# Two layers of a hybrid decoder trunk on one core: another order of the setup, an output tail by row blocks, and a later place for one small sum

## The reference, cut to what matters

```python
for l in range(2):                                   # 512 tokens, 1024 channels
    mod = silu(c) @ ada_w[l] + ada_b[l]              # 9 rows of 1024: shift, scale, gate, three times
    h = rms_norm(x, ffn1_norm[l]) * (1 + sc1) + sh1
    x = x + 0.5 * g1 * ((silu(h @ Wg) * (h @ Wu)) @ ffn1_w_out[l])
    h = rms_norm(x, mix_norm[l]) * (1 + sc2) + sh2   # 8 heads, two softmax maps each, with a
    ...                                              # relative bias; conv of 31 taps; two gates
    x = x + g2 * (merged @ w_mix_out[l])
    h = rms_norm(x, ffn2_norm[l]) * (1 + sc3) + sh3
    x = x + 0.5 * g3 * ((silu(h @ Wg) * (h @ Wu)) @ ffn2_w_out[l])
return rms_norm(x, final_norm)
```

## Time and profile before

| | |
|---|---|
| runs | 2573.01, 2574.42, 2575.19 us (median 2574.42) |
| profiled execution | 2577.65 us, its span 2576.0 us |
| PE busy in the span | 2514.0 us |
| DVE, ACT, POOL busy | 1675.6, 966.4, 115.8 us |
| chain that ended last, PE's share | 84% |

### The profile page before, as it was taken

One profiled execution on the slowest core, in us unless ns is written; L12 is line 12 of the kernel. 1 busy time (PEld: TensorE's weight loads), 2 busy tenths in 40 slices (PEclk: granted clock), 3 DMA queues, 4 the chain that ended last, 5 costly groups with the idle time before them and its releaser, 6 DMA issues.

```text
span 2576.0 us, 34560 instructions
## 1 busy us (share of the span) xinstructions
PE 2514.0 (98%) x11378; PEld 2033.8 (79%) x11378; DVE 1675.6 (65%) x2493; ACT 966.4 (38%) x1625; POOL 115.8 (4%) x186
## 2 busy tenths in 40 slices
PE   5899999999999999999999999999999999999997
PEld 4788887777778888888878888877777888788886
DVE  6555578798988675543365557778989865643333
ACT  3222323545444343232243232255455443423222
POOL 2100010000000000000000001100000000000000
PEclk7899999999999999999999999999999999999998
DMA  6655475232232334543335555722232233333332
GB/s 215 182 161 157 148 237 160 81 87 82 84 89 83 101 120 131 161 125 93 103 89 158 161 163 188 228 78 84 83 87 80 86 98 98 90 94 95 96 96 94
DMA packets 470157, 311.97 MB, mean 121 GB/s; under 512 B 10723, under 2 KB 447205, under 8 KB 470084
## 3 DMA queue, kind: packets, MB, share of 16 engines
q1 hardware_dynamic: 445078, 227.63, 30.4%
q0 software_dynamic: 22144, 78.40, 9.4%
q10 hardware_dynamic: 2878, 5.20, 0.7%
HBM read 306.46 MB, written 5.05 MB: 121 GB/s over the span
## 4 chain that ended last, share of the span: by engine, by line
PE 84%; DVE 8%; issue 3%; ACT 3%; DMA 1%; ACTq 0%; POOL 0%; DVEq 0%; POOLq 0%; SPq 0%
PE bank L1307 26%; PE bank L1309 25%; PE bank L1308 25%; PE bank L1498 2%; DVE ada_acc L853 1%; PE bank L1477 1%; ACT w_hi L418 1%; DVE rstd L732 1%; DVE w_lo L715 1%; PE bank L1469 1%; DVE scaled L743 1%; DVE h_lo L752 1%; PE bank L1329 1%; DMA bias_rows<-bias_row 1%; PE bank L1334 0%
## 5 line engine op out<-in xcount | busy, mean ns | idle before, releaser
L715 DVE TENSOR_TENSOR w_lo<-w_raw,w_hi 128x1024 fp32r<-128x1024 f32 (+1 forms) x432 | 520.0, 1204 | 562.9 <-ACT w_hi L418 562.4
L1307 PE MATMUL bank<-h_hi,w_hi 128*128 128x512 f32 x2112 | 840.0, 398 | 9.1 <-DVE scaled L993 9.0
L1309 PE MATMUL bank<-h_hi,w_lo 128*128 128x512 f32 x2112 | 824.1, 390 | 0.0
L1308 PE MATMUL bank<-h_lo,w_hi 128*128 128x512 f32 x2112 | 823.8, 390 | 0.0
L418 ACT ACTIVATE w_hi<-w_raw 128x1024 fp32r<-128x1024 f32 (+1 forms) x432 | 449.5, 1041 | 864.1 <-PE bank L1309 807.0
L1307 PEld LDWEIGHTS bank<-h_hi,w_hi 128*128 128x128 f32 x2112 | 397.3, 188 | 100.2 <-issue 18.8
L1309 PEld LDWEIGHTS bank<-h_hi,w_lo 128*128 128x128 f32 x2112 | 397.0, 188 | 84.3
L1308 PEld LDWEIGHTS bank<-h_lo,w_hi 128*128 128x128 f32 x2112 | 397.7, 188 | 77.9 <-issue 0.5
L1097 DVE SCALAR_TENSOR_TENSOR conv_part<-glu,conv_taps,conv_part 128x512 f32<-128x512 f32 x464 | 318.9, 746 | 0.0
L1307 PE MATMUL bank<-s_hi,w_hi 128*128 128x512 f32 x704 | 274.6, 390 | 0.0
L1309 PE MATMUL bank<-s_hi,w_lo 128*128 128x512 f32 x704 | 274.0, 389 | 0.0
(11 more groups left out here) (199 smaller groups left out, 2535.1 us busy)
## 6 DMA issues: line engine op xcount, KB each, us to landing
w_raw<-in_ffn_w_in SPq DMA_DIRECT2D x176, 512.0 KB, 3.8
ada_raw<-in_ada_w POOLq DMA_DIRECT2D x128, 512.0 KB, 4.9
w_raw<-in_w_mix_in SPq DMA_DIRECT2D x112, 512.0 KB, 3.7
w_raw<-in_ffn_w_out SPq DMA_DIRECT2D x64, 512.0 KB, 3.8
w_raw<-in_ffn_w_out SPq DMA_DIRECT2D x32, 384.0 KB, 3.4
w_raw<-in_w_mix_out SPq DMA_DIRECT2D x18, 512.0 KB, 3.7
ada_first<-in_ada_w POOLq DMA_DIRECT2D x16, 512.0 KB, 10.8
w_raw<-in_w_attn_branch SPq DMA_DIRECT2D x16, 512.0 KB, 3.8
```

Source lines behind the costliest of these rows:

```text
L715: dve.tensor_tensor(wlo[slot][:, 0:n, :], raw[slot][:, 0:n, :], whi[slot][:, 0:n, :].bitcast(F32), ALU.subtract).then_inc(w_lo[slot], 1)
L1307: pe.matmul(acc, wh, hi[:, k0 + k, :], start=first and k == 0, stop=False)
L1308: pe.matmul(acc, wh, lo[:, k0 + k, :], start=False, stop=False)
L1309: mm = pe.matmul(acc, wl, hi[:, k0 + k, :], start=False, stop=last and k == n - 1)
```

## The change

Five things move:

- **POOL** issues all 16 pieces of `ada_first` and the lambda rows in one run, with no wait for `w_raw` between them; `row_rstd` comes behind them. The bias rows no longer wait for `lam_dots`.
- **Setup order.** PE turns the rows of x first, and makes the bias rows behind them; DVE does its two steps for that table (`bias_table`) after its fourth `first_step`. ACT splits the first two slabs ahead of `running_sum`. PE does `first_sum(0)` ahead of `norm_mean`. DVE splits slab 0 behind `scale_columns`.
- **ACT** waits for the bias rows and issues its two DMAs behind the whole tile loop of the first FFN; the copy itself is awaited only behind the norm of the mixing stage.
- **Group sums** in `ffn1_out` stand before block 5 of slab 5.
- **Tail.** The last `ffn2_out` is written out four times instead of a loop. In it ACT multiplies each finished tile of x by the gain (`out_gain`), PE turns it (`turn_rows`, 7 tiles within the slabs), ACT copies it (`out_copy`), all without the norm. The mean squares come as one column per 128 tokens: PE multiplies blocks of `running_sum` by a column of 1/1024 (`token_sums`), and behind the last slab those of the last square. ACT takes the root of 128x4, DVE the reciprocal, DVE and ACT scale the rows by it, and SP writes four DMAs of 512 KB. The unused last pair is gone.

```diff
 @@ gpsimd
             pool.dma_start(ADA0[:, k, D:2 * D], w_ada[:, k, D:2 * D]).then_inc(sem(f"ada0_scale{k}"), 16)
-        pool.wait_ge(sem("minus_half"), 1)
-        pool.wait_ge(sem("row_var"), 1)
-        pool.tensor_tensor(row_rstd[:, :], row_var[:, :], minus_half[:, :].to_broadcast([P, QB]), ALU.pow)\
-            .then_inc(sem("row_rstd"), 1)
-        for s in range(2):
-            pool.wait_ge(w_raw[s], 16)
         for k in range(KT):
             pool.dma_start(ADA0[:, k, 0:D], w_ada[:, k, 0:D]).then_inc(sem(f"ada0_shift{k}"), 16)
...
+        pool.wait_ge(sem("minus_half"), 1)
+        pool.wait_ge(sem("row_var"), 1)
+        pool.tensor_tensor(row_rstd[:, :], row_var[:, :], minus_half[:, :].to_broadcast([P, QB]), ALU.pow)\
+            .then_inc(sem("row_rstd"), 1)
...
         pool.wait_ge(sem("ada0_step"), 2 * KT)
-        pool.wait_ge(sem("lam_dots"), 2 * DEPTH)
         pool.wait_ge(sem("br_copied"), 2)
 @@ scalar
+        for s in range(2):
+            w_hi_part(0, s)
         act.wait_ge(sem("ssum_clear"), 1)
         act.wait_ge(sem("row_rstd"), 1)
         for t in range(QB):
             act.activation(SSUM[:, t * P:(t + 1) * P], ident[:, :], ACT.Copy, scale=row_rstd[:, t:t + 1]).then_inc(sem("row_sums"), 1)
-        for s in range(2):
-            w_hi_part(0, s)
...
                 ffn_tile(1, False, TP[0])
+                with act.Fori(2, FT) as i:
+                    ffn_tile(i)
                 if l == 0 and w == 0:
                     act.wait_ge(sem("br_out"), 16 * HEADS)
...
-                with act.Fori(2, FT) as i:
-                    ffn_tile(i)
...
+                            if last:
+                                out_gain(i * 2 + m // 3)
...
+                        if last and m == 5:
+                            out_copy(i * 2)
+                        if last and m == 2 and i:
+                            out_copy(i * 2 - 1)
 @@ tensor
+        def turn_rows(j):
+            pe.wait_ge(sem("y_gained"), j + 1)
+            if j >= 2:
+                pe.wait_ge(sem("y_copied"), j - 1)
+            for t in range(QB):
+                mm = pe.transpose(TP[j % 2][:, t * P:(t + 1) * P], T[j % 2][:, t * P:(t + 1) * P], ident[:, :])
+            mm.then_inc(sem("yt_ready"), 1)
+        def token_sums():
+            pe.wait_ge(sem("ssum_add"), DEPTH * 3 * KT - 1)
+            for t in range(QB):
+                pe.matmul(AUX[:, t:t + 1], SSUM[:, t * P:(t + 1) * P], invd[:, 0:1], start=t == 0, stop=False)
...
+                    if w == 0:
+                        extra[5] = {5: lambda: mod_sum_parts(seq + 1)}
+                    if last:
+                        extra[4] = {2: lambda: turn_rows(i * 2)}
+                        if i:
+                            extra[1] = {2: lambda: turn_rows(i * 2 - 1)}
+                        if i == KT // 2 - 1:
+                            extra[5] = {4: token_sums}
...
-                             at={2: lambda: mod_sum_parts(seq + 1)} if w == 0 and m == 5 else {})
+                             at=extra.get(m, {}))
```

More of the change, by code:

```diff
@@ L328, in _ @@
                             slab(pair + PAIR0[name] + i, t, cols(wt, l * KT, 8, i * (2 * P) + t * P + c0))
-        for s in range(2):
[L331 to L339, removed]
-        for s in range(2):
-            sp.wait_ge(w_raw[s], 16 * (DEPTH * PAIRS + 1))
+        for n in range(QB):
+            t = n // 2 + 2 * (n % 2)
+            sp.wait_ge(sem("y_last"), QB)
+            sp.wait_ge(sem(("y_scaled_dve", "y_scaled_act")[n % 2]), n // 2 + 1)
+            sp.dma_start(out[0, t * P:(t + 1) * P, :], YO[:, t, :]).then_inc(sem("y_out"), 16)
+        sp.wait_ge(sem("y_out"), 16 * QB)
     @block.gpsimd
@@ L507, in _ @@
             plain_hi(0, j)
+        act.wait_ge(sem("aux_ready"), 1)
+        act.activation(RSTD[:, :], AUX[:, :], ACT.Copy, scale=float(D)).then_inc(sem("aux_read"), 1)
         for s in range(2):
@@ L543, in _, with out_pair @@
                     load_bias_tile(0)
-                with act.Fori(2, FT) as i:
-                    ffn_tile(i)
-                if l == 0 and w == 0:
                     act.wait_ge(sem("lam_dots"), 2 * DEPTH)
-                    act.wait_ge(sem("br_again"), 16)
                     act.activation(lam_exp[:, :], lam_dot[:, :], ACT.Exp).then_inc(sem("lam_exps"), 1)
-                with act.Fori(0, KT // 2) as i:
+                last = l * 3 + 1 + 2 * w == DEPTH * 3
+                def out_pair(i):
                     for m in range(6):
@@ L699, in _ @@
                         plain_hi(l * 3 + 2, i * 2 + t)
[L702 to L706, removed]
+        act.wait_ge(sem("y_means"), 1)
+        act.activation(yroot[:, :], AUX[:, 0:QB], ACT.Sqrt, bias=eps[:, 0:1]).then_inc(sem("y_root"), 1)
+        act.wait_ge(sem("y_rstd"), 1)
+        for t in (2, 3):
+            act.activation(YO[:, t, 0:D - P], YO[:, t, 0:D - P], ACT.Copy, scale=yrstd[:, t:t + 1]).then_inc(sem("y_scaled_act"), 1)
         act.wait_ge(sem("bt_in"), 16 * (DEPTH * HEADS + 1))
@@ L1046, in _, with out_pair @@
                 clear_sum()
-                with dve.Fori(0, KT // 2) as i:
+                last = l * 3 + 1 + 2 * w == DEPTH * 3
+                def out_pair(i):
                     for m in range(6):
@@ L1068, in _ @@
                         chunk_columns(l, i * 2 + (4 + 2 * CHUNKS_IN[0]), seq + 1)
+                if last:
+                    for i in range(KT // 2):
+                        out_pair(i)
+                else:
+                    with dve.Fori(0, KT // 2) as i:
+                        out_pair(i)
                 if w == 1:
@@ L1415, in _ @@
         first_sum(0).then_inc(sem("scale0_summed"), 1)
+        norm_mean(0, 0)
         pe.wait_ge(sem("pt_ready"), 1 + DEPTH)
@@ L1455, in _ @@
                              k0, OUTG[g], g == 0, g == 2,
-                             at={2: lambda: mod_sum_parts(seq + 1)} if w == 0 and m == 5 else {})
+                             at=extra.get(m, {}))
+                if last:
+                    for i in range(KT // 2):
+                        out_pair(i)
+                else:
+                    with pe.Fori(0, KT // 2) as i:
+                        out_pair(i)
                 if w == 1:
@@ L1579, in _ @@
                              ready=lambda k: pe.wait_ge(sem("m_lo"), l * KT + k + 1))
-        norm_mean(DEPTH * AUXN, DEPTH * 3 * KT)
-        for j in range(KT):
-            pe.wait_ge(sem("unit_t"), DEPTH * UNITS + j + 1)
-            if j >= 2:
-                pe.wait_ge(sem("y_ready"), j - 1)
-            for t in range(QB):
-                mm = pe.transpose(TP[j % 2][:, t * P:(t + 1) * P], T[j % 2][:, t * P:(t + 1) * P], ident[:, :])
-            mm.then_inc(sem("yt_ready"), 1)
+        pe.wait_ge(sem("sq_ready"), DEPTH * 3 * KT)
+        for t in range(QB):
+            mm = pe.matmul(AUX[:, t:t + 1], SQ[:, t * P:(t + 1) * P], invd[:, 0:1], start=False, stop=t == QB - 1)
+        mm.then_inc(sem("y_means"), 1)
+        turn_rows(KT - 1)
     ctx.close()
```

101 lines of the change are left out of this document (65 added, 36 removed).

## The result

The changed kernel takes **2561.7 us** (median of 5 runs, 2560.63 to 2562.82) against 2574.47 of the kernel before; the ratio is 0.9949, with a 95% interval of 0.9936 to 0.9963. In time that is 13.1 us less (9.5 to 16.5), where 17.2 were forecast: the forecast time, 2557.2, missed by 4.5 us, and the range of 2552 to 2563 holds the measured one. The profiled execution took 2561.09 us, its span 2559.4.

What follows compares the result with a forecast made beforehand. PE, with 84% of the chain, was taken as the bound. Setup plus 4.1, stall minus 10.7, group sums minus 4.2 and tail minus 6.4 gave minus 17.2: 2574.4 to 2557.2 us, range 2552 to 2563 (8 in 10: 2549 to 2567).

Steps and rivals of the forecast that it cites:

- The stall: First FFN: PE's 8.1 us wait goes, and the low clock behind it (2.6 us): minus 10.7 us.
- The setup: Setup: the shift's 4096-byte packets starve the first slabs' 512-byte ones, `h_hi` starts at 38.9, not 34.80: plus 4.1 us.
- the last 0.08 MB take 0.3 us: Setup: after the shift's end at 35.1 us, SP's queue finishes slot 1's data by 35.4; semaphore at 36.6.
- The rule named in the prediction: Skill's DMA page: each DMA engine takes queues in turn by packet, not bytes; by it the sum is minus 17.2 us.
- The group sums: `ffn1_out`: sums three blocks later no longer wait, 8 times 0.53 us: minus 4.2 us.
- The tail: Last `ffn2_out` and end: PE gets 4.05 us more, the end comes 10.5 us sooner: minus 6.4 us.
- The 17.2: Whole kernel: the us saved by the sum of setup, stall, group sums and tail, from 2574.4 to 2557.2 us.
- The two signs of the setup: Setup: ACT's second `w_hi` starts at 36 to 37 us with a wait for `w_raw`; `h_hi` at about 39.
- no wait of over 1 us: Sign of being right: PE has no wait over 1 us between the shift's sums and the tail.
- B: Rival, setup: first slabs not starved, `h_hi` at some 31.8 us, setup minus 3.0, sum minus 24.3, 2550 us; chance 0.13.
- C: Rival, first FFN: the stall moves, as a slab beside the bias rows lands late; 2562 to 2568 us; chance 0.17.
- D: Rival: PE's clock stays low behind the shift's sums; decides from 86 matmuls, at 150 plus 13, 2587 us; chance 0.02.

Runs made afterwards that it cites:

- the second execution: The kernel before, unchanged, profiled a second time: ratio 0.9999 (0.9989 to 1.0008), span 2574.9 us.

## Why the prediction was right, and where it was off

**The stall, forecast minus 10.7.** Right in sum. The table has minus 10.94 against the profiled execution, of which 8.1 are the wait and the rest the low clock behind it. But that execution had a longer stall than the other four that have one (14.79 against 12.77 to 13.27 us), so the usual gain there is 8.9 to 9.4, and the part alone measured minus 10.0 (6.4 to 13.6). What the prediction had not told apart is which edit does it. It is POOL's `lam_dots` wait: moved alone, it removes the stall (minus 9.0), and putting ACT's wait back costs nothing once POOL issues early. The third edit, ACT's wait for `br_again` behind the stage, guards against a new wait: without it 2.3 us are lost in `ffn1_out`.

**The setup, forecast plus 4.1.** The mechanism was right, equal packets and unequal bytes, and it was the only part that costs time; the term was undersized, at plus 5.8 in the traces and plus 5.7 (3.3 to 8.0) alone. The step that was off is "the last 0.08 MB take 0.3 us", with the 1.2 us behind it (their row gives 1.1): it let SP's queue run free once the shift was through, at 35.1, and took the 16 DMA engines as one. The queues from 35 to 36 us:

```profile
DMA packets 338, 0.26 MB, mean 259 GB/s; under 512 B 80, under 2 KB 261, under 8 KB 338
q0 software_dynamic: 153, 0.17, 79.8%
q1 hardware_dynamic: 185, 0.09, 41.2%
```

POOL's queue still held packets: the lambda rows stand in its list behind the shift, 0.26 MB in all that the trace has as 128 packets of 2048 bytes, and the sum had left them out. At the 385 GB/s of this stage they are some 0.7 us, an estimate. But slot 1 was there only at 38.59, its split came at 38.61 and not at 36.6, and the trace shows more. The slab's semaphore is raised 16 times, once for each part, in the changed kernel first at 35.01, four times by 35.3, and for the last eight parts from 37.8 to 38.59. On the average the sum was good: before 36 us SP's queue had started as many packets as both slabs have. But the parts ended 3.6 us apart (3.9 with the setup part alone), and packets of the next slab, issued at 31.05, already went out before slot 1 was there. With the shift kept back they ended 1.2 us apart. So beside the shift the queue moves on unevenly, and a slab counts when its last part is there. Why it is uneven, and how the 2 us divide between this and the lambda rows, no run shows. From the split to `h_hi` it took 2.13 us, 2.3 forecast.

The true size may be larger still. Against the five runs in which the old setup has its first slab at 35.13 to 35.79, the setup part's 42.45 is 6.7 to 7.3 us later, within the interval of its run alone.

The rule named in the prediction, from the Trainium skill's page DMA: Bandwidth & Descriptors, section Queues, rings and completion order (queues take turns by packet), agrees with the counts wherever all queues have work: 566 and 564 with two queues, 484, 479 and 481 with three. The page's packet is a group of descriptors; whether the profile counts the same thing is not shown.

**The group sums, forecast minus 4.2.** Minus 4.2 in the table (2.0 and 2.2), minus 4.1 (1.8 to 6.4) alone. The time from start to start was the right measure; the table of waits had shown 1.8.

**The tail, forecast minus 6.4.** PE got 4.4 us more in the last `ffn2_out` (4.05 forecast), and the end came 11.05 us sooner (10.5 forecast): minus 6.65, or minus 6.4 against the second execution. The part alone measured minus 5.9 (3.3 to 8.2). The first output DMA came 5.4 us behind the start of the last matmul, 5.5 by the prediction's sum.

**The sum.** Trace against trace it came out at minus 16.6, and at minus 15.5 against the second execution. The four parts alone add up to 5.7 - 10.0 - 4.1 - 5.9 = -14.3. The medians of the whole differ by 12.8, its ratio gives 13.1 (9.5 to 16.5), and the run with ACT's wait in its old place, which is the same in time, gave 13.9. So of the 4.5 us by which 2557.2 missed, 1.7 are the undersized setup and up to 1.8 a stall read from one execution in which it was longer than usual; the rest is within what the measurement can tell. The 17.2 itself lies just outside the measured 9.5 to 16.5. The prediction's range is also not quite what its bounds give: with plus 2 to plus 6, 1.8 to 4.2 and minus 4 to minus 8 it is 2553.5 to 2563.9, which holds the result as well.

**The signs.** The group sums, the end and the missing stall came as said. The two signs of the setup did not: the second `w_hi` at 38.61 and not at 36 to 37, `h_hi` at 40.74 and not at about 39. And "no wait of over 1 us" behind the shift's sums overlooked the 1.8 us for `shift_parts`, which is in both kernels.

**The rivals.** B was wrong for this kernel, and near to what the new order is worth once the slabs are not starved: it gave minus 24.3, and POOL's old order in the changed kernel measured minus 22.9, with `h_hi` at 30.34 instead of B's 31.8. Part of why is a thing the prediction passed over: before, `h_hi` waited 5.02 us for `norm_scale`, and the new order on DVE has it ready at 29.1. C did not come: the longest wait of PE behind the shift's sums is the 1.8 us that were there before. The time alone would not have told: 2561.7 stands at the edge of C's 2562 to 2568. D did not come either: behind the shift's sums seven slab matmuls stand 0.43 us apart, the last of them at 73.42 us, and from 74.25 on it is 0.23 again; D needed 86.

## What to carry to other kernels

In all stretches read here, DMA queues that had work shared by packets and not by bytes: ask of each load that could go out earlier how long its packets are, and whose short ones they will stand beside. Keeping the shift's 4.19 MB back until about 28 us, or giving an urgent slab a queue of its own, was worth 8.5 to 10.3 us here, by ratios whose intervals are some 3.5 us to either side; the first slab came 7.6 to 10.4 us sooner. And an operation that another engine waits for must not stand in a list behind a row of DMA issues: with the shift kept back alone, half of the gain went into that (4.7 us of 9.8 were left).

Read a stall's length in more than one execution before it is entered in a sum: 14.79 us in one was 12.8 to 13.3 in four.

## What the runs showed of the hardware

A third queue did not raise the total, but moved the shares: 373 GB/s with three queues from 15 to 21 us, 385 GB/s with two in the same stretch, while the slabs' part rose from 0.27 to at least 0.46 MB in 6 us. The Trainium skill's page DMA: Bandwidth & Descriptors, in its section Rules for kernel authors, says that spreading DMAs over the issuing engines does not help bandwidth and only saves issue time. Of the total this trace agrees. The share of one urgent load is another matter: it rose, and the run was 8.5 us faster than the changed kernel.

A load over all 16 DMA engines ends when its last part does, and beside a stream of 4096-byte packets the parts of a slab of 512-byte packets ended 3.6 us apart, against 1.2 us in the run with the shift kept back.

Packets of 512 bytes nearly alone did not reach the rate of mixed ones. From 22.5 to 24 us of the run with the shift kept back, the DMA engines are busy throughout (the share is over 100% because packets' times overlap):

```profile
DMA packets 876, 0.45 MB, mean 298 GB/s; under 512 B 16, under 2 KB 874, under 8 KB 876
q1 hardware_dynamic: 871, 0.44, 113.3%
```

That is 298 GB/s, against 385 GB/s while 4096-byte packets ran beside them (15 to 21 us of the changed kernel).
